# A decoder layer on one core: four projection fills made in thirds between the turns of the x tiles

## What is computed

```python
hn = rms_norm(x, norm_mix[0])        # x * rsqrt(mean(x*x) + 1e-6) * gain, row by row
proj = hn @ w_in                     # 2048x1024 @ 1024x3072: q, k and v
q, k, v = jnp.split(proj, [D, 2 * D], axis=-1)
```

## Time and profile before

| what | us |
|---|---|
| median of 3 runs | 2501.5 |
| lowest and highest of them | 2501.24 and 2504.43 |
| the profiled execution's own time | 2500.24 |
| the span of its profile | 2498.7 |

### The profile page before, as it was taken

One profiled execution on the slowest core, in us unless ns is written; L12 is line 12 of the kernel. 1 busy time (PEld: TensorE's weight loads), 2 busy tenths in 40 slices (PEclk: granted clock), 3 DMA queues, 4 the chain that ended last, 5 costly groups with the idle time before them and its releaser, 6 DMA issues. The chain is left out here.

```text
span 2498.7 us, 36865 instructions
## 1 busy us (share of the span) xinstructions
PE 2297.3 (92%) x11480; PEld 1843.1 (74%) x11480; DVE 1382.9 (55%) x2803; ACT 1209.7 (48%) x1636; POOL 761.7 (30%) x686
## 2 busy tenths in 40 slices
PE   4999999998999999999979997599999999999980
PEld 3888888997667676766658886477888888788760
DVE  6212121002877777777635776577655565666763
ACT  5111111112777777777743443475545464655653
POOL 0000000001887777777700111222222222222220
PEclk8999999999999999999989998799999999999995
DMA  5333334223643544354135455589887878888957
GB/s 194 135 109 118 126 118 145 68 64 86 157 101 90 133 106 102 84 121 118 30 117 201 128 138 179 203 296 356 288 286 234 286 228 285 304 291 287 319 151 286
DMA packets 207630, 441.46 MB, mean 177 GB/s; under 512 B 19082, under 2 KB 56114, under 8 KB 205491
## 3 DMA queue, kind: packets, MB, share of 16 engines
q1 hardware_dynamic: 188530, 379.46, 45.9%
q0 software_dynamic: 19008, 60.91, 9.7%
HBM read 338.55 MB, written 101.76 MB: 176 GB/s over the span
## 5 line engine op out<-in xcount | busy, mean ns | idle before, releaser
L1446 DVE TENSOR_TENSOR gu_lo<-gu_raw,gu_hi 128x2048 fp32r<-128x2048 f32 x128 | 293.3, 2291 | 119.9 <-issue 83.0
L573 POOL TENSOR_TENSOR p_ring<-p_ring 128x512 f32<-128x512 f32 (+2 forms) x192 | 334.6, 1743 | 16.0
L633 DVE TENSOR_SCALAR_CACHE_REDUCE p_ring<-ps_s 128x512 f32<-128x512 f32 (+6 forms) x352 | 276.9, 791 | 98.0 <-PE ps_s L704 88.5
L598 ACT ACTIVATE p_ring<-p_ring,shift 128x1152 f32<-128x1152 f32 (+15 forms) x256 | 305.8, 1197 | 21.9 <-DVE shift L649 21.9
L741 PE MATMUL ps_o<-aT,v_st 128*128 128x512 f32 (+3 forms) x640 | 285.5, 530 | 0.0
L587 ACT ACTIVATE aT<-ps_t 128x512 f32<-128x512 f32 (+1 forms) x320 | 168.9, 530 | 168.7 <-PE ps_t L726 167.5
L1523 PE MATMUL ps_g<-gu_hi,xT_lo 128*128 128x512 f32 x720 | 235.9, 409 | 8.2 <-DVE xT_lo L1461 8.2
L1386 ACT ACTIVATE gu_hi<-gu_raw 128x2048 fp32r (+1 forms) x128 | 237.9, 1916 | 9.2 <-PE ps_g L1523 4.8
L1523 PE MATMUL ps_g<-gu_lo,xT_hi 128*128 128x512 f32 x720 | 227.4, 397 | 0.0
L1523 PE MATMUL ps_g<-gu_hi,xT_hi 128*128 128x512 f32 x720 | 227.3, 397 | 0.0
L570 POOL TENSOR_SCALAR p_ring<-p_ring,coef 128x512 f32<-128x512 f32 (+2 forms) x192 | 168.1, 875 | 129.8 <-DVE coef L662 127.8
(11 more groups left out here) (217 smaller groups left out, 4363.8 us busy)
## 6 DMA issues: line engine op xcount, KB each, us to landing
gu_raw<-in_moe_w_gate SPq DMA_DIRECT2D x128, 512.0 KB
gu_raw<-in_moe_w_up SPq DMA_DIRECT2D x128, 512.0 KB
d_raw<-in_moe_w_down SPq DMA_DIRECT2D x64, 1024.0 KB
qk<-stage SPq DMA_DIRECT2D x64, 512.0 KB, 2.8
q_first<-qk SPq DMA_DIRECT2D x64, 256.0 KB, 5.0
q_second<-qk SPq DMA_DIRECT2D x64, 256.0 KB, 5.1
w_raw<-in_diff_w_in POOLq DMA_DIRECT2D x12, 1024.0 KB, 6.8
k<-qk SPq DMA_DIRECT2D x8, 1024.0 KB, 12.2
```

The costliest lines, as they stand in the source:

```text
L573: pool.tensor_tensor(p0(r, c0, c1), p0(r, c0, c1), p1(r, c0, c1), ALU.add).then_inc(mixed, 1)
L598: nc.scalar.activation(p, p, ACT.Exp, bias=shift[:, r % 8, m:m + 1], accum_out=sums[:, r % 8, m:m + 1]).then_inc(raised, 1)
L633: ins = nc.vector.tensor_scalar(p(r, k0, k0 + far), ps_s[:, c % 2, 0:far], SCALE, None, ALU.mult, ALU.max, accum_out=top[:, r % 4, m, col: ...
L1446: nc.vector.tensor_tensor(gu_lo[:, j * GC:(j + 1) * GC], raw(half, j), gu_hi[:, j * GC:(j + 1) * GC].bitcast(F32), ALU.subtract).then_inc( ...
```

## The change

The first term of a fill needs only the rounded part of four tiles, and fills 0 to 3 of the first block need only the first half of the tokens once the order of fills is changed: a block's fill `n` now takes token group `n // 2` and column half `n % 2` (before: group `n % 4`, half `n // 4`). With that order:

- PE's list: each of the turns 4 to 15 is followed by one third of a fill (one term, eight matmuls), which makes fills 0 to 3 complete in twelve thirds. Behind the last turn come two flips, fill 4, two flips, and fills 5, 6 and 7. All later blocks are as before.
- PSUM: two places for turned tiles in place of three (banks 0 to 3), so turn `t` waits for the rest of tile `t - 2`; fill `n` goes to bank `(n + 4) % 8`. The squares go to a part of `hnT_lo` that is written last, and the flips use banks 2 and 3 twice.
- ACT: a square root of a single number per row at the very start (`warm`), one square root for each of tiles 0 to 3, and three tiles measured ahead of the first copy in place of six; the lead grows back to five.
- DVE: the first weight split moves from the front of its list to behind the second tile; the second split moves between the copies of the flips' results, and the first two blocks' takes are written out.

The core of the diff (left out: the rotated bank numbers in the takes and in the v blocks, and the loops that call the same pieces for the later blocks):

```diff
+        eps, warm = sb("eps", [P, 1]), sb("warm", [P, 1])
+        junk = hnT_lo[:, :, (TILES - 1) * P:]
...
-        MEASURED = 6
+        AHEAD = (3, 5, 7, 8)
...
-            return ps[:, (t % 3) * 2:(t % 3) * 2 + 2, :].rearrange("p a (b t) -> p (a b) t", t=P)
+            return ps[:, (t % 2) * 2:(t % 2) * 2 + 2, :].rearrange("p a (b t) -> p (a b) t", t=P)
+
+        def roots(g):
+
+            return 4 + g
+
+        def ahead(t):
+
+            return AHEAD[t] if t < len(AHEAD) else AHEAD[-1] + t - len(AHEAD) + 1
...
-                    dst = scratch["qk"][bass.ds(b * 2 + n // 4, 1)].rearrange("o h p t -> p (o h) t")
-                    sp.dma_start(dst[:, :, (n % 4) * 512:(n % 4) * 512 + 512],
+                    dst = scratch["qk"][bass.ds(b * 2 + n % 2, 1)].rearrange("o h p t -> p (o h) t")
+                    sp.dma_start(dst[:, :, (n // 2) * 512:(n // 2) * 512 + 512],
...
-                nc.scalar.activation(ps[:, 6:8, :].rearrange("p a b -> p (a b)"), x_tile(g, i), ACT.Square,
+                nc.scalar.activation(junk, x_tile(g, i).rearrange("p (c e) -> p c e", c=KC), ACT.Square,
                                      accum_out=sumsq[:, g % 2, i:i + 1]).then_inc(squared, 1)
-                if i == 3:
+                if g == 0 or i == 3:
+                    own = slice(i, i + 1) if g == 0 else slice(0, 4)
                     act.wait_ge(squared, t + 1 + SQUARED0)
...
-            for t in range(MEASURED):
+            nc.scalar.activation(warm[:, :], eps[:, :], ACT.Sqrt, bias=eps[:, 0:1], scale=1.0)
+            for t in range(AHEAD[0]):
                 measure(t)
...
-                if t + MEASURED < TILES:
-                    measure(t + MEASURED)
+                for u in range(ahead(t), min(ahead(t + 1), TILES)):
+                    measure(u)
...
-            split(0, 0)
...
             for t in range(TILES):
                 dve.wait_ge(hn_hi, t + 1)
+                if t >= TILES - 1:
+                    dve.wait_ge(squared, TILES + SQUARED0)
...
+                if t == 1:
+                    split(0, 0)
-            dve.wait_ge(flipped, 2)
             for k in range(4):
-                nc.vector.tensor_copy(unskewed[:, k * 512:(k + 1) * 512], ps[:, (2, 3, 6, 7)[k], :]).then_inc(z_set, 1)
+                if k == 2:
+                    split(1, 1, 0)
+                dve.wait_ge(flipped, 2 + k // 2)
+                nc.vector.tensor_copy(unskewed[:, k * 512:(k + 1) * 512], ps[:, 2 + k % 2, :]).then_inc(z_set, 1)
+            take_block(0, 0)
+            split(2, 0, 8)
+            take_block(1, 8)
...
+            def term(half, n, k):
+                w, h = TERMS[k]
+                for c in range(KC):
+                    mm = pe.matmul(ps[:, (n + 4) % 8, :], w[:, half, c, (n % 2) * P:(n % 2 + 1) * P],
+                                   h[:, c, (n // 2) * 512:(n // 2 + 1) * 512], start=k == 0 and c == 0,
+                                   stop=k == 2 and c == KC - 1)
+                if k == 2:
+                    mm.then_inc(filled, 1)
+
+            def first_term(n, k):
+
+                if n == 0 and k == 0:
+                    pe.wait_ge(w_split, 2)
+                    pe.wait_ge(z_set, 2)
+                if n % 2 == 0 and k == 0:
+                    pe.wait_ge(hn_hi, n // 2 * 4 + 4)
+                if n % 2 == 0 and k == 1:
+                    pe.wait_ge(hn_lo, n // 2 * 4 + 4 + HN_LO0)
+                term(0, n, k)
...
-                if t >= 3:
-
-                    pe.wait_ge(hn_lo, t - 2 + HN_LO0)
+                if t >= 2:
+
+                    pe.wait_ge(hn_lo, t - 1 + HN_LO0)
...
+                if t >= 4:
+
+                    first_term((t - 4) // 3, (t - 4) % 3)
...
-            pe.wait_ge(hn_lo, 14 + HN_LO0)
-            pe.wait_ge(squared, TILES + SQUARED0)
-            for k in range(4):
-                mm = pe.matmul(ps[:, (2, 3, 6, 7)[k], :], flip[:, :], skewed[:, k * 512:(k + 1) * 512], start=True, stop=True)
-            mm.then_inc(flipped, 1)
-            pe.wait_ge(hn_lo, TILES + 2)
+            for n in range(4, 8):
+                if n < 6:
+                    pe.wait_ge(z_set, 3 + 2 * (n - 4))
+                    for k in range(2):
+                        q = 2 * (n - 4) + k
+                        mm = pe.matmul(ps[:, 2 + k, :], flip[:, :], skewed[:, q * 512:(q + 1) * 512], start=True, stop=True)
+                    mm.then_inc(flipped, 1)
+                if n == 6:
+                    pe.wait_ge(z_set, 7)
+                for k in range(3):
+                    first_term(n, k)
```

More of the change, by code:

```diff
@@ L208, in _ @@
                 for n in range(8):
-                    take(b * 8 + n + 1, n, b * 32 + 16 * (n // 4), stage[:, n % 4, 0:512], ps[:, n, :])
+                    take(b * 8 + n + 1, n, b * 32 + 16 * (n // 4), stage[:, n % 4, 0:512], ps[:, (n + 4) % 8, :])
             act.wait_ge(out_lo, BANKS + QK_FILLS)
@@ L214, in _ @@
                     act.wait_ge(stored[n % 4], b * 64 + (QKB * 32 + 16 * (n // 4) + 1))
-                    nc.scalar.activation(stage[:, n % 4, 0:WB].bitcast(F32), ps[:, n % 8, 0:WB], ACT.Copy).then_inc(out_lo, 1)
+                    nc.scalar.activation(stage[:, n % 4, 0:WB].bitcast(F32), ps[:, (n + 4) % 8, 0:WB], ACT.Copy).then_inc(out_lo, 1)
         @block.vector
@@ L235, in scale @@
                 g, i = t // 4, t % 4
-                if i == 0:
-                    dve.wait_ge(rooted, g + 1)
+                if g == 0 or i == 0:
+                    own, done = (slice(i, i + 1), i + 1) if g == 0 else (slice(0, 4), roots(g))
+                    dve.wait_ge(rooted, done)
                     if g >= 2:
                         dve.wait_ge(normed, (g - 1) * 4 + NORMED0)
-                    nc.vector.reciprocal(rstd[:, g % 2, :], root[:, g % 2, :]).then_inc(inverted, 1)
-                    dve.wait_ge(inverted, g + 1 + INVERTED0)
+                    nc.vector.reciprocal(rstd[:, g % 2, own], root[:, g % 2, own]).then_inc(inverted, 1)
+                    dve.wait_ge(inverted, done + INVERTED0)
                 nc.vector.scalar_tensor_tensor(out=x_tile(g, i), in0=x_tile(g, i), scalar=rstd[:, g % 2, i:i + 1],
@@ L258, in take, with take_block @@
                 nc.vector.tensor_tensor(dst, src, hi.bitcast(F32), ALU.subtract).then_inc(out_lo, 1)
-            split(0, 0)
+            def take_block(b, first):
+                for n in range(8):
+                    take(first + n + 1, stage[:, n % 4, 512:1024], stage[:, n % 4, 0:512], ps[:, (n + 4) % 8, :])
             scale(0)
@@ L268, in _ @@
                     scale(t + 2)
-            dve.wait_ge(flipped, 2)
+                if t == 1:
+                    split(0, 0)
             for k in range(4):
-                nc.vector.tensor_copy(unskewed[:, k * 512:(k + 1) * 512], ps[:, (2, 3, 6, 7)[k], :]).then_inc(z_set, 1)
-            with dve.Fori(0, QKB // 2) as b2:
+                if k == 2:
[5 more added lines that the diff above has]
+            take_block(1, 8)
+            with dve.Fori(1, QKB // 2) as b2:
                 for half in range(2):
                     split(b2 * 2 + half + 1, 1 - half, b2 * 16 + half * 8)
-                    for n in range(8):
-                        take(b2 * 16 + half * 8 + n + 1, stage[:, n % 4, 512:1024], stage[:, n % 4, 0:512], ps[:, n, :])
+                    take_block(b2 * 2 + half, b2 * 16 + half * 8)
             for b in range(VB):
@@ L325, in _, with block_of @@
+            def block_of(b, half, first):
+                pe.wait_ge(w_split, b + 2)
+                for n in range(8):
+                    pe.wait_ge(out_lo, first + n + 1)
+                    for k in range(3):
+                        term(half, n, k)
+            block_of(1, 1, 8)
+            with pe.Fori(1, QKB // 2) as b2:
+                for half in range(2):
+                    block_of(b2 * 2 + half, half, b2 * 16 + half * 8)
             with pe.Fori(0, VB // 2) as b2:
```

27 lines of the change are left out of this document (6 added, 21 removed).

## The result

The changed kernel takes 2482.32 us (median of four runs, 2480.24 to 2484.09), the kernel before beside it 2501.56 (four runs, 2501.24 to 2504.43): a ratio of 0.9923, with a 95% interval of 0.991 to 0.9935. That is 19.2 us, faster by 0.8%. The profiled execution is the slowest of the four, 2484.09, with a span of 2482.5.

The account below looks back on a forecast made before the run. PE, busy 92% of the span, bounds the kernel. Four fills leaving its row give 22.2 us, less 2.9 for flips and 1.5 for the head's later end: 17.8 gained, 2501.5 to 2483.7; range 2479.7 to 2489.5.

Parts of the forecast that it names:

- The start, up to turn 4: Start of the head: turn 0 at 13.0 instead of 20.3, turn 4 at 30.0 instead of 31.6.
- Turns and thirds: Head from turn 4: PE without gaps, 2.68 us a step at 2.4 GHz, 5.07 at 1.2 GHz.
- rival 1: Head: DVE and ACT set the pace, costing 6.7 us together; 2487 to 2491, chance 0.15.
- Rival 4: Behind 93.3 us something waits for other than PE, so no gain at the end; 2501.5, chance 0.01.
- the clock's instant: Head: PE's clock rises to 2.4 GHz at 38.0, by choice; each us later costs 0.47 of gain.
- the case at the low end of the forecast's own range: Head: clock rises with the first third at 31.6; fill 5 at 72.5, gain 20.8, low end 2480.7.
- Rivals 2 and 3: Head: clock rises and falls as now, 2500.2 to 2504, chance 0.05; or stays at 1.2 GHz, 2507 to 2511, chance 0.04.
- The end of the head: After the last rest: two flip pairs of 1.72 on PE's row, 2.9 us more; fill 5 at 75.5.
- behind it PE has the same row of work in both kernels: Everything after fill 5 starts: PE's work is unchanged, so the gain measured at that instant carries through.
- from there every row about 18 earlier: Sign of being right: from fill 5 near 75.5 on, all rows come about 18 us earlier.
- The rule against the change: Head: the skill says transposes don't engage full clock, so only the thirds would count and 1.2 GHz could stay.

Follow-up runs that it names:

- e5: The changed kernel with the first weight split one place earlier, ahead of DVE's first rest: 2478.54 us, ratio 0.9911.
- e1: The changed kernel with fills 0 to 3 made behind the last turn, nothing between the turns: 2501.63 us, ratio 1.0005.
- e7: The kernel before with two places for turned tiles instead of three: 2501.17 us, ratio 1.0.
- e3: The changed kernel run again, unchanged, for a second trace: 2482.67 us, ratio 0.9921.
- e8: e5 with 38 more semaphore increments at the front of DVE's list: 2478.35 us, ratio 0.9897.
- e10: The kernel before with 26 semaphore increments at the front of DVE's list: 2503.09 us in one run.
- e2: The changed kernel with the start of the kernel before (one root for four tiles, split first, two table loads): 2483.22 us, ratio 0.9927.

## Why the prediction held, point by point

The predicted 2483.7 is 1.4 above the median of 2482.3, and of the rivals none came true. Under that small difference two errors of about 2 us each lie, with opposite signs; that they cancel is luck.

**The start, up to turn 4,** held: turn 0 at 13.16 (13.0 predicted), turn 4 at 29.24 (30.0). Of the 0.8, half is ACT's second copy, in front of which I put the square and root of tile 3 and the square of tile 4 at the pitches of the old rows: its rest began at 20.56, not 21.0. The other half are DVE's steps behind it, each a little shorter; the split ended at 26.64, not 27.2. That the split "now lies on the path" is what e5 shows from the other side: off it, turn 4 is 2.53 earlier.

**Turns and thirds** held in both steps. At 2.4 GHz the step is 2.71, for 2.68 predicted; the changes of kind cost 0.03 a tile, against bounds of zero and 0.23. The third at 1.2 GHz, which no row of before had and which I took as 3.5 between 1.81 and 3.62, is 3.56 in e1 and in e5. DVE and ACT follow: no row of PE between 32 and 62 us has a gap (30.00 of 30.00), so rival 1 (DVE and ACT set the pace) fell with its price of 6.7. Rival 4 (no effect at the end of the kernel) fell with the median. DVE's margin is small as predicted, with idle times of 0.3 per tile ahead of the rests. The third place costs nothing (e7).

**The step that was mis-sized is the clock's instant,** which I set by choice to 38.0. It rose within the first third: that took 2.62 from matmul to matmul, between 1.94 at full clock and 3.56 at the low one, so by my estimate it ran 1.5 us of it at the low clock (1.5/3.56 + 1.1/1.94 = 1.0), and the rise is at 30.86 + 1.5, some 32.4. By the 0.47 that the prediction gives for each us, the 5.6 us are 2.6 of gain, and the case at the low end of the forecast's own range (a rise at 31.6, rest done at 63.6, fill 5 at 72.5, gain 20.8) is close to what the trace shows: 64.01, 72.67, 20.6. In e3, the same kernel, the same working puts the rise at 33.9 and the gain of it at 1.9, with the rest done at 64.93 and fill 5 at 73.61; so the size of this error differs from one execution to the next. Rivals 2 and 3 (the clock goes up and down, or stays at 1.2 GHz) fell: 1.00 from 32 to 62.

**The end of the head** held: the flips wait for the last rest (0.53), fill 4 starts 65.48 - 64.06 = 1.42 behind them, fill 5 another 5.87 + 1.32 later; the prediction had 1.72, 5.44 and 1.72. The pairs are cheaper and the fill behind a pair dearer; together 8.61 for 8.88.

**What fell is the sentence "behind it PE has the same row of work in both kernels",** and with it "from there every row about 18 earlier". In the rows of the projection it is so: 20.6 at fill 5, 20.2 at the start of the v blocks. Then attention is 1.5 longer and experts 0.8, which by e8 and e10 is the place of DVE's code: 26 more instructions in front of it. The second mis-sized term is therefore one that the sum didn't have. 20.2 less 2.3 is 17.9. The medians say 19.2, the two profiled executions 16.2; the stages that vary from run to run, by 2.1 and 6.4 us, cover both.

**The rule against the change** is the Trainium skill's, "TensorE: Matmul & The Clock Gate", Part 4, that full clock doesn't engage for transposes. The trace before had a rise after nothing but turns. e1 shows the same once more: from turn 0 to 61.22 its PE has done only turns, and its windows give a mean of 0.57 from 38 to 62, more than the 0.50 of the low clock alone. In the changed kernel the clock stays at 1.00 with thirds between the turns; that the thirds hold it there rather than the row being closed no run here separates.

## What to carry to other kernels

Work that waits behind a latency-bound stage is worth most of its length when it is put into that stage's gaps on the engine that bounds the rest: four fills of 5.44 moved, and the projection ended 18.0 us earlier with the old start (e2) and 20.2 with the new. The earlier start of the same stage gave nothing until the gaps were filled (e1), and 1.3 to 2.2 us at fill 5 after that, by single profiles. An operation that moves out of an idle gap onto the path, as the split did here, should be looked for in the trace of the changed kernel; putting it back into the next gap gave another 3.8 us in the median (2482.3 to 2478.5, e5), though the end of the projection shows only 1.6 or 2.6 of it, against the two profiles of the changed kernel. When a loop that wasn't touched becomes longer by 0.2%, compare its "issue" rows with those of the kernel before: the number of instructions ahead of it may be all that has changed. That undoing it pays in the time of the whole kernel isn't shown (e8's median against e5's).
